# The first model's layers in another order: where the key's root, the masks, the latent values and the router's matmuls stand

## The reference, cut to what matters

```python
for l in range(2):                                   # first model
    h = rmsnorm(x) * (1 + scale) + shift
    proj = h @ w_in[l]                               # 4512 columns
    y_a = rwkv7_branch(...)                          # delta rule over 8 heads
    y_b = mla_branch(...)                            # latent attention, 8 heads
    merged = sigmoid(g_a) * y_a + sigmoid(g_b) * y_b
    x = x + gate * (merged @ w_o[l])
    x = x + gate * (swiglu(h) if l == 0 else moe_swiglu(h))   # 8 experts, top 2
# rwkv7: kk = kk * rsqrt(sum(kk * kk)); y = ((y - mu) * rsqrt(var)) * lnx_g + lnx_b
#        y = (y + bonus) * gate; y_a = y @ rwkv_out
# mla:   q = rmsnorm(q_a) @ w_qb; kv = rmsnorm(kv_a) @ w_kvb; the last 32 dims of q and k are rotated
#        o = softmax(q k^T, by chunks) v;  y_b = o @ mla_out
```

## Time and profile before

| | |
|---|---|
| median of 3 runs | 2949.95 us (2945.87 to 2951.54) |
| profiled execution, own time | 2941.82 us |
| its span | 2940.2 us |
| PE busy | 2833.6 us, 96% |
| DVE busy | 722.7 us, 25% |
| ACT busy | 489.0 us, 17% |
| POOL busy | 233.2 us, 8% |
| chain that ended last, by engine | PE 67%, SP's queue 23%, issue 6%, DVE 2%, ACT 1% |
| read from HBM | 629.82 MB, 215 GB/s over the span |

### The profile page before, as it was taken

How to read it: one execution, slowest core, us unless ns; L and a number is a source line. 1 busy time by engine, 2 the same in 40 slices (tenths; PEclk the granted TensorE clock), 3 DMA queues, 4 the chain that set the end, 5 groups by cost and what they waited for, 6 DMA issues and landing times.

```text
span 2940.2 us, 49988 instructions
## 1 busy us (share of the span) xinstructions
PE 2833.6 (96%) x20416; PEld 1872.1 (64%) x20416; DVE 722.7 (25%) x1713; ACT 489.0 (17%) x1007; POOL 233.2 (8%) x410
## 2 busy tenths in 40 slices
PE   7999999999988999999999999999999999999999
PEld 5777788887867432322222222277888888878888
DVE  4422454434243101011101101135520002632000
ACT  3213210032232100000000000014420003350000
POOL 4000000000000122222222121200000000000000
PEclk9999999999998999999999999999999999999999
DMA  9562378732220999999999999933343434333442
GB/s 299 163 196 95 101 252 275 259 111 81 67 86 29 353 362 374 375 378 372 378 371 378 370 385 368 362 117 120 115 138 120 166 125 140 120 113 123 150 159 85
DMA packets 435572, 634.18 MB, mean 216 GB/s; under 512 B 29802, under 2 KB 244992, under 8 KB 435216
## 3 DMA queue, kind: packets, MB, share of 16 engines
q1 hardware_dynamic: 406544, 600.97, 59.1%
q10 hardware_dynamic: 26400, 28.76, 3.0%
q0 software_dynamic: 2400, 1.26, 0.2%
HBM read 629.82 MB, written 1.05 MB: 215 GB/s over the span
## 4 chain that ended last, share of the span: by engine, by line
PE 67%; SPq 23%; issue 6%; DVE 2%; ACT 1%; DMA 1%; ACTq 0%; DVEq 0%
PE bank L524 47%; SPq L2808 20%; PE accum L524 19%; SPq L2794 2%; DVE w L1920 1%; SPq L2735 1%; PE bank L643 1%; DMA ring<-in_ada_w_dram 0%; ACT L1430 0%; DMA ring<-in_moe_w_dram 0%; PE bank L1084 0%; ACT sh L1430 0%; PE bank L880 0%; DVE h L1926 0%; ACT h L1430 0%
## 5 line engine op out<-in xcount | busy, mean ns | idle before, releaser
L524 PE MATMUL bank<-h,ring 128*128 128x256 f32 (+1 forms) x3712 | 824.4, 384 | 11.0 <-ACT w L1430 5.0
L524 PEld LDWEIGHTS bank<-h,ring 128*128 128x128 f32 (+1 forms) x3712 | 703.8, 192 | 120.3 <-issue 17.3
L524 PE MATMUL bank<-w 64*64 64x64 f32 (+3 forms) x4146 | 283.5, 332 | 13.0 <-DVE w L1920 6.2
L524 PE MATMUL bank<-ring,w 128*32 (+1 forms) x1742 | 240.9, 592 | 0.0
L524 PEld LDWEIGHTS bank<-w 64*64 64x64 f32 (+2 forms) x4146 | 148.2, 131 | 144.9 <-issue 131.7
L524 PE MATMUL accum<-w,ring 128*128 128x256 f32 x1056 | 233.2, 379 | 0.0
L524 PE MATMUL bank<-w,ring 128*128 128x256 f32 x1024 | 226.7, 382 | 4.8 <-DVE w L1920 3.9
L524 PEld LDWEIGHTS accum<-w,ring 128*128 128x128 f32 x1056 | 200.5, 190 | 27.6 <-issue 0.4
L524 PEld LDWEIGHTS bank<-w,ring 128*128 128x128 f32 x1024 | 194.3, 191 | 33.1 <-DVE w L1920 5.5
L1920 DVE TENSOR_TENSOR w<-bank,w 128x256 f32<-128x256 f32 (+1 forms) x114 | 61.2, 537 | 532.3 <-ACT w L1430 524.3
L524 PEld LDWEIGHTS bank<-ring,w 128*32 128x32 f32 x1742 | 67.0, 110 | 160.4 <-issue 160.4
(11 more groups left out here) (327 smaller groups left out, 2408.7 us busy)
## 6 DMA issues: line engine op xcount, KB each, us to landing
ring<-in_moe_w_dram SPq DMA_DIRECT2D x816, 256.0 KB, 7.7
w<-in_moe_w_dram SPq DMA_DIRECT2D x528, 256.0 KB, 7.6
ring<-in_w_in_dram SPq DMA_DIRECT2D x76, 1024.0 KB, 5.2
ring<-in_w_ffn_in_dram SPq DMA_DIRECT2D x44, 1024.0 KB, 5.2
ring<-in_ffn_w_dram SPq DMA_DIRECT2D x33, 1024.0 KB, 7.8
ring<-in_ada_w_dram SPq DMA_DIRECT2D x24, 1024.0 KB, 11.3
w<-in_ada_w_dram ACTq DMA_DIRECT2D x24, 1024.0 KB, 5.9
ring<-in_w_ffn_out_dram SPq DMA_DIRECT2D x22, 1024.0 KB, 4.8
```

The costliest lines, as they stand in the source:

```text
L524: ins = nc.tensor.matmul(o, lhsT, rhs, start=start, stop=stop, skip_group_check=skip)
```

## The change

In each layer of the first model: the logs of kk's sums go to i == 8 ahead of the powers on ACT, the exponential of the root behind them. DVE masks RB and RK ahead of both `first_level`s. One R moves from FILL_END to the second FILL_HALF (the order of the loads follows, since SP reads the same strings). The rotation of the key goes ahead of the queries on PE and DVE. DVE forms (bonus + lnx_b) * gate and y * lnx_g * gate early and finishes yT with two products ahead of the heads; the multiplication of the queries by the cosine is split in two halves and put ahead of the sine products. The scores of heads 0 and 1 are issued ahead of the values vn_ (a new argument `first` of `attention`), the copies of the values follow the exponentials of heads 0 and 1, and each head has one ya tile. In both models each merged tile signals by itself, and the first tile of the output projection waits for them one by one (`parts`). In the router, two groups of transposes and lam go behind the ranks.

The diff, cut: context is left out, and so are the new parameter in the signature of `attention`, the calls `project(("wo", l), 8, mrg1, ..., merged)` and the same for wo2 in place of one wait for `merged`, ACT's counts of fill tiles to drain, and the second model's merge, changed as the first's.

```diff
@@ -122,12 +122,12 @@
-FILL_OPS, FILL_HALF, FILL_LEVEL = "RR", ("RMM", "RMM"), ("MMR", "MMR", "MMR", "MMR", "MM")
-FILL_CHUNK, FILL_END = ("R", "RM", "RM"), "RRMM"
+FILL_OPS, FILL_HALF, FILL_LEVEL = "RR", ("RMM", "RRMM"), ("MMR", "MMR", "MMR", "MMR", "MM")
+FILL_CHUNK, FILL_END = ("R", "RM", "RM"), "RMM"
...
-YA_AT = [[], [], [0], [1], [2], [3], [4, 5], [6, 7]]
+YA_AT = [[m] for m in range(8)]
...
@@ -631,6 +631,8 @@
                 scores_ahead(1)
+                if first:
+                    first()
...
@@ -752,7 +754,13 @@
-            def project(tag, kt, src, pair=None):
+            def project(tag, kt, src, pair=None, parts=None):
+                def part(at, k):
+                    if parts and at == 0:
+                        pe.wait_ge(parts, next_of("merged"))
+                    return src[:, k, :]
...
@@ -760,7 +768,7 @@
                         t, f = take(tag + (at,))
-                        contract(t[:, 0:T], kt, lambda k: w(k, m * P, m * P + P), lambda k: src[:, k, :]).then_inc(f, 1)
+                        contract(t[:, 0:T], kt, lambda k: w(k, m * P, m * P + P), lambda k: part(at, k)).then_inc(f, 1)
...
@@ -873,21 +881,20 @@
-                for a in range(TT):
-                    for g in range(2):
-                        t, f = take(("hnat", a, g))
-                        for i in range(4):
-                            ins = nc.tensor.transpose(t[:, i * P:(i + 1) * P], h[:, g * 4 + i, a * P:(a + 1) * P], ident)
-                        ins.then_inc(f, 1)
-                        if a == g == 0:
-                            pe.wait_ge(*read_out(("logit_parts",)))
-                            t, f = take(("logits",))
-                            for b in range(TT):
-                                ins = mm(t[:, 8 * b:8 * b + 8], logit_parts[:, b * P:(b + 1) * P], c("pick_q", 0, 8), last=True)
-                            ins.then_inc(f, 1)
-                pe.wait_ge(lam_prod, next_of("lam_prod"))
-                t, f = take(("lam",))
-                mm(t[:, 0:4], ones[0:64, :], small[0:64, 0:4], last=True).then_inc(f, 1)
+                def turned_tokens(a, g):
+                    t, f = take(("hnat", a, g))
+                    for i in range(4):
+                        ins = nc.tensor.transpose(t[:, i * P:(i + 1) * P], h[:, g * 4 + i, a * P:(a + 1) * P], ident)
+                    ins.then_inc(f, 1)
+                turned_tokens(0, 0)
+                pe.wait_ge(*read_out(("logit_parts",)))
+                t, f = take(("logits",))
+                for b in range(TT):
+                    ins = mm(t[:, 8 * b:8 * b + 8], logit_parts[:, b * P:(b + 1) * P], c("pick_q", 0, 8), last=True)
+                ins.then_inc(f, 1)
+                turned_tokens(0, 1)
...
@@ -895,6 +902,11 @@
                 mm(t[:, 16:24], ones[:, :], router["sel"](1), False, True, last=True).then_inc(f, 1)
+                for g in range(2):
+                    turned_tokens(1, g)
+                pe.wait_ge(lam_prod, next_of("lam_prod"))
+                t, f = take(("lam",))
+                mm(t[:, 0:4], ones[0:64, :], small[0:64, 0:4], last=True).then_inc(f, 1)
...
@@ -1216,6 +1228,8 @@
                 pe.wait_ge(qnormed, next_of("qnormed"))
+                t, f = take(("krot", l))
+                mm(t[0:96, 0:T], c("rot96")[0:96, :], qa[0:96, 5, :], last=True).then_inc(f, 1)
...
@@ -1231,8 +1245,6 @@
                     turned_query(hd)
-                t, f = take(("krot", l))
-                mm(t[0:96, 0:T], c("rot96")[0:96, :], qa[0:96, 5, :], last=True).then_inc(f, 1)
...
@@ -1242,33 +1254,49 @@
                     ins.then_inc(f, 1)
-                for a in range(TT):
-                    t, f = take(("vn_", l, a))
-                    contract(t[:, 0:512], 2, lambda k: qa[:, 3 + k, a * P:(a + 1) * P],
-                             lambda k: w(k, 0, 1024).rearrange("p (g e) -> p g e", e=P)[:, :, 64:128]).then_inc(f, 1)
-                release.append(s)
...
                         return
-                    if hd == 2:
+                    if hd == 0:
...
+                def latent_value(hd, kt):
+                    if hd == 0 and kt == 0:
+                        pe.wait_ge(*read_out(("vn_", l, 1)))
+                    return mvn[:, kt, hd * 64:hd * 64 + 64]
+                def latent_values():
+                    for a in range(TT):
+                        t, f = take(("vn_", l, a))
+                        contract(t[:, 0:512], 2, lambda k: qa[:, 3 + k, a * P:(a + 1) * P],
+                                 lambda k: w(k, 0, 1024).rearrange("p (g e) -> p g e", e=P)[:, :, 64:128]).then_inc(f, 1)
+                    release.append(s)
                 pe.wait_ge(roped, next_of("roped"))
-                pe.wait_ge(*read_out(("vn_", l, 1)))
-                attention(("mla", l),
-                          lambda u, a: qrot[0:96, u, a * P:(a + 1) * P],
+                pe.wait_ge(*read_out(("kn_", l, 0)))
+                def roped_query(u, a):
+                    if u == 2 and a == 0:
+                        pe.wait_ge(*read_out(("kn_", l, 3)))
+                    if u == 4 and a == 0:
+                        pe.wait_ge(roped, next_of("roped"))
+                    return qrot[0:96, u, a * P:(a + 1) * P]
+                attention(("mla", l), roped_query,
                           lambda u, n: krot[0:96, u, 0:n],
-                          lambda hd, kt: mvn[:, kt, hd * 64:hd * 64 + 64],
-                          lambda hd: slice(64 * (hd % 2), 64 * (hd % 2) + 64), take_upper, out_tiles)
+                          latent_value,
+                          lambda hd: slice(64 * (hd % 2), 64 * (hd % 2) + 64), take_upper, out_tiles, latent_values)
...
                 project(("yb", l), 4, oT1)
-                pe.wait_ge(merged, next_of("merged"))
-                project(("wo", l), 8, mrg1, norm_sums(("n2", l), take_upper, True))
+                project(("wo", l), 8, mrg1, norm_sums(("n2", l), take_upper, True), merged)
...
@@ -1442,7 +1469,7 @@
-            def root_by_log(keys, buf, n, eps):
+            def logs(keys, buf, n, eps):
...
@@ -1450,9 +1477,18 @@
+            def root_of_logs(keys, buf):
...
                     act.wait_ge(*read_out(key))
+                at = sum(w for _, w in keys)
...
+            def root_by_log(keys, buf, n, eps):
+                logs(keys, buf, n, eps)
+                root_of_logs(keys, buf)
...
@@ -1644,12 +1680,13 @@
                     elif i == 8:
+                        kk_sums = [(("kk", l, 0), 2), (("kk", l, 1), 2)]
+                        logs(kk_sums, rsk, 1, 2)
...
                         fn(ppr[:, :, :], ppr[:, :, :], ACT.Exp, scale=-DECAY).then_inc(powers_ready, one("powers_ready"))
-                    elif i == 10:
-                        root_by_log([(("kk", l, 0), 2), (("kk", l, 1), 2)], rsk, 1, 2)
+                        root_of_logs(kk_sums, rsk)
...
@@ -1676,7 +1713,7 @@
                 copy_out(("MV", l, 1), MV[:, 1, :])
-                drain_rest(1)
+                drain_rest(2)
...
@@ -1723,11 +1760,14 @@
                         ins.then_inc(reader_of(("kn_", l, hd // 2)), 1)
-                for a in range(TT):
-                    act.wait_ge(*full(("vn_", l, a)))
-                    nc.scalar.activation(mvn[:, a, :], psum_of(("vn_", l, a))[:, 0:512], ACT.Copy
-                                         ).then_inc(reader_of(("vn_", l, a)), 1)
-                attention(("mla", l))
+                def latent_values(hd):
+                    if hd < TT:
+                        act.wait_ge(*full(("vn_", l, hd)))
+                        nc.scalar.activation(mvn[:, hd, :], psum_of(("vn_", l, hd))[:, 0:512], ACT.Copy
+                                             ).then_inc(reader_of(("vn_", l, hd)), 1)
+                attention(("mla", l), latent_values)
...
@@ -2389,12 +2429,12 @@
                 masked(("M", l, 1), M4, c("strict"))
-                first_level(0)
...
                 dve.wait_ge(*full(("MV", l, 1)))
-                first_level(1)
+                for a in range(TT):
+                    first_level(a)
...
@@ -2447,22 +2487,6 @@
                 dve.wait_ge(*read_out(("yl", l, NCH - 1)))
-                for g in range(2):
-                    dve.wait_ge(*full(("ymean", l, g)))
-                    t = psum_of(("ymean", l, g))
-                    y = yT[:, 2 * g:2 * g + 2, :]
-                    stt(y, t[:, 0:512].rearrange("p (j t) -> p j t", t=T), -1.0 / 64, y, MUL, ADD).then_inc(reader_of(("ymean", l, g)), 1)
-                dve.wait_ge(*read_out(("ymean", l, 1)))
-                for hd in range(8):
-                    dve.wait_ge(*full(("qrot", l, hd)))
-                    t = psum_of(("qrot", l, hd))
-                    tt(qsin[0:96, hd, :], t[0:96, 0:T], rope[0:96, 1, :], MUL).then_inc(reader_of(("qrot", l, hd)), 1)
-                dve.wait_ge(*read_out(("q", l, 7)))
```

(56 more changed lines are left out.)

10 lines of the change are left out of this document (4 added, 6 removed).

## The result

The changed kernel takes 2906.83 us (median of 4 runs, 2906.49 to 2911.58) beside 2949.5 us (median of 4 runs, 2945.87 to 2951.54) for the kernel before: a ratio of 0.9859 [0.9848, 0.9871], 42.7 us less. Forecast were 2909.6 us and 40.3 us less. The profiled execution took 2911.58 us (span 2909.8), so it is the slowest of the four.

A forecast was written before the change was run, and what follows sets the result against it. TensorE, busy 96% of the span, was taken as the bound, so its idle or half-clock time counts. 5.0 + 8.4 + 22.3 + 3.6 + 1.0 = 40.3 us off the 2949.95 us median gave 2909.6 us, range 2899 to 2927.

The forecast's parts named there:

- Part 1: Key root: logs ahead of powers on ACT free the banks early, ending PE's 2.48 us wait a layer; 5.0 us.
- Part 2: Inverse's setup: masks ahead of first levels, a fill tile moved to cover them; 8.4 us over both layers.
- The ring of SyncE's queue: Load order changes with the fill; a modulation load may come 0 to 4 us late in layer 0, taken as 0.
- Rival (b): Load ring or instruction delivery takes back part, or attention starts 2 us late a layer: 32 won, 2918 us; chance 0.14.
- The late weights of M7: Layer 0's inverse: this modulation piece's load waits for a slot released about 150 us, wanted at 157; up to 4 us.
- Part 3: Latent attention: reordering fills PE's gaps and restores 2.4 GHz; 11.4 us in layer 0, 10.9 in layer 1, 22.3 together.
- the added wait: Latent attention's turned queries: DVE starts draining later, at 278.7 instead of 277.23, after half a cosine product; 1.5 us.
- (a): Latent attention's clock does not recover: idle time won, half-clock time not; 29.2 us won, 2921 us; chance 0.18.
- (c): Latent stretch of both layers runs at 1.2 GHz: costs 84 us in all, 2994 us; chance 0.03.
- Part 4: Four output projections: waiting for merged tiles singly removes a 0.98 us wait, taken as 0.9 each; 3.6 us.
- Part 5: Router: ranks' matmuls start after four transposes instead of twelve and lam, so routing and experts' DMA start 1.0 us earlier.

The follow-up runs named there:

- part 2 alone undone: Masks' order and fill tile as before, against the changed kernel: 2911.99 us, ratio 0.9869.
- light loads: Changed kernel with layer 0's second modulation loading an eighth of its bytes, same matmuls: 2900.07 us, ratio 0.9828.
- second pair of executions: The same two kernels profiled again without edit: changed 2912.03 us (ratio 0.9863), the kernel before 2949.23 us (ratio 0.9994).
- eight pieces moved: Changed kernel with eight of twelve modulation pieces moved from the inverse's levels to the chunks: 2904.61 us, ratio 0.9848.
- all twelve: Changed kernel with all modulation pieces in the chunk loop: 2901.79 us, ratio 0.9826; once more 2900.81 us, ratio 0.983.

## Why the prediction was right, step by step

| part | forecast | measured |
|---|---|---|
| 1, key root | 5.0 | 5.5 (2.74 a layer) |
| 2, masks and fill, layer 0 | 3.9 | -2.8 (-1.8 to -3.8 over the pairs; part 2 alone undone: -1.3 and -1.5) |
| 2, layer 1 | 4.55 | 4.2 (3.5 to 4.95; part 2 alone undone: 5.4 and 6.7) |
| 3, latent attention | 22.3 | 23.3 (22.3 to 24.3) |
| 4, merged tiles | 3.6 | 5.0 (1.24 each) |
| 5, router | 1.0 | 1.0 and 1.6 |

In part 2 the key's rotation, which now stands ahead of the queries, is taken off (0.5 us a layer). Parts 1, 4 and 5 were not undone one by one; their sizes are differences of stages.

The measured parts sum to about 36.5 us, 34.0 of them ahead of the experts, where 38.5 were forecast. The medians differ by 42.7 us in the first comparison and by 38.4 in the second. So the time was right, and one term of the sum was not. That the medians come so near to 40.3 is in part luck. The profiled executions are only 30.4 and 33.5 us apart: those of the kernel before were 7.7 and 1.4 us below its medians, those of the changed one 4.8 and 2.5 above. The traces say where such differences can lie, in the expert stage and in the clock of the second model, and not what the executions without a trace did.

**Part 1** came as forecast: both waits for ACT are gone, and the banks' reader is done before PE gets there.

**Part 2 is the step that failed**, in layer 0: "The ring of SyncE's queue ... I take 0", with the gain of 3.9 behind it. The mechanism of the gain was right: without the stalls the masks' order is worth 6.7 us by stages, its old form brings back exactly the 2.62 us, and in layer 1 the gain is there. But PE arrives earlier at levels full of short products while the M pieces load, and there it stops for 7.0 us instead of the 3.7 us that the same stretch had before, and runs 2 x 3.4 us at half clock, which no part of the levels did. That is 3.3 us of waits, and 3.4 us more since 6.8 us at half clock do the work of 3.4. Of the first pair of executions, where layer 0 stands at -3.6, these 6.7 us are most of the 7.5 between 3.9 and -3.6. The other 0.8 is in the masks: without the wait of 1.07 us the fill would begin 3.05 us earlier than before, not 3.9. The loss itself, and that it hangs on the bytes loaded at the time, is shown (61.1 to 53.0 us with light loads, no such wait with the loads elsewhere). That the path is the delivery of PE's instructions is argued from the packets' times, from the equal distance of the waits in PE's program and from the wait in products that read no weights; I had no kernel that changes that queue alone. Rival (b) held this mechanism at "1 to 2 us amid the inverse's levels" and a loss of 4, without the half clock. The late weights of M7, its other reason for that loss, don't show as a wait for a load in the levels. Its other arm, attention's start late by 2 us a layer, did not come: the first transposes stand at 289.87, forecast 290.7.

**Part 3** followed its steps: the added wait was 0.54 us (1.5 forecast), the first transposes 13.4 us after the first turned query (14), a head 3.71 us (3.71), yb 41.4 us after it (42.9). The full clock came back once the gaps were filled, as the earlier trace rows had suggested, and went again where the old order was put back (0.61 and 0.66). By the Trainium skill (TensorE: Matmul & The Clock Gate, "The HAM clock gate") activity releases the throttled state, and this stretch at 1.00 agrees. Rivals (a) and (c) fell with it. The smaller gain of the second pair of executions (22.3 us) comes from the kernel before, which there took 66.2 instead of 68.1 us in layer 0 from the start of the queries to yb; the changed one took 55.73 in both layers.

**Part 4** was too small: the wait was 0.98 us, the gain is 1.24 each. From yb to the sums of the next norm it took 42.79 us and now 41.55. What the remaining 0.26 us is, was not tried; PE's restart after the wait is a guess. Little of this gain is left at the end of the two profiled executions: the feed-forward part of layer 0 takes 1.3 and 1.1 us more than before, and the second model 2.9 and 3.2 us more beside the 2.5 that it wins, each with more time at half clock. Other kernels with the same edit don't have all of it (245.1 to 248.6 us for that feed-forward part, 247.3 before), so it varies with the execution or with what stands ahead; which, was not tried.

**Part 5** is at its size: from the norm's sums to the experts' first product 20.12 us before, 19.07 and 18.47 now. The chain was the one forecast, but the ranks' matmuls now wait for DVE (1.55 and 1.10 us), which the sum had as no wait.

Within the sum errors cancelled in part: 6.7 us too much in part 2, 0.35 more in layer 1, against 0.5, 1.0, 1.4 and up to 0.6 too little in the others. The rest, from 36.5 us to the medians' 38.4 and 42.7, no trace accounts for.

## What to carry to other kernels

When a wait is removed, look at what PE then runs into earlier: short matmuls beside a full DMA queue can stall without a releaser, and the half clock that can come behind such a stall costs as much again. Waits without a releaser that sit in a kernel before are a price to be put into the sum, and the heaviest loads belong where PE issues few matmuls in a microsecond (eight pieces moved so gained 4.9 us in layer 0's stage, all twelve 10.5). Where a change is worth less than the variation of a long stage, put landmarks ahead of that stage and judge by them, in two executions of each kernel. When a stage that no edit touches has changed, look at its clock first. And when a forecast made from one execution meets a median, ask how far that execution was from its own median.
